# One value group a step, a fourth score bank and the maxima ahead of the copies, in the attention stage of a two-block model on one Trainium2 core

## What is computed, as far as it matters here

```python
def masked_softmax(s, mask):
    s = jnp.where(mask, s.astype(jnp.float32), -jnp.inf)
    m = jnp.max(s, axis=-1, keepdims=True)
    m = jnp.where(jnp.isfinite(m), m, 0.0)
    e = jnp.exp(s - m)
    den = jnp.sum(e, axis=-1, keepdims=True)
    return e / jnp.where(den > 0, den, 1.0)
o = gb[..., 0:1] * ocb + gb[..., 1:2] * o_sel + gb[..., 2:3] * o_win
```

## Time and profile before

| | |
|---|---|
| runs | 1525.81 us median of 3 (1525.8 to 1526.4) |
| the profiled execution | 1525.48 us, of which 1523.7 us from its first to its last instruction |
| granted TensorE clock | 1.00 |
| busy | PE 1499.2 us (98%), DVE 1067.5, ACT 697.7, POOL 272.8 |
| the stage of the change | from about 662 to 817 us of the span |
| two steps in the middle of it | 18.1 us, PE busy all of it |

### The profile page before, as it was taken

The page is one execution under the profiler, slowest core; times in us unless marked ns, Lnnn a source line. Parts: engine busy times, 40 slices in busy tenths (PEclk is TensorE's granted clock), DMA queues, the critical chain, the costliest instruction groups (busy, mean ns, idle before and its releaser), DMA issues.

```text
span 1523.7 us, 21005 instructions
## 1 busy us (share of the span) xinstructions
PE 1499.2 (98%) x8228; PEld 1247.5 (82%) x8228; DVE 1067.5 (70%) x1619; ACT 697.7 (46%) x1209; POOL 272.8 (18%) x206
## 2 busy tenths in 40 slices
PE   6999999999999999999999999999999999999999
PEld 5788888888888897987878888888888898877777
DVE  6898688889988773268885685666534653688665
ACT  4453552322314454357775552322314443777761
POOL 0110013223232000059872011111100011010000
PEclk9999999999999999999999999999999999999999
DMA  9775257468585213330000255344332342112211
GB/s 340 259 263 176 84 215 259 169 247 305 185 285 185 87 53 132 122 116 2 2 2 29 83 196 171 115 141 166 139 111 83 97 156 83 56 55 65 86 72 56
DMA packets 114248, 207.54 MB, mean 136 GB/s; under 512 B 6361, under 2 KB 21990, under 8 KB 114150
## 3 DMA queue, kind: packets, MB, share of 16 engines
q1 hardware_dynamic: 113822, 206.09, 39.4%
q10 hardware_dynamic: 328, 0.12, 0.0%
HBM read 202.00 MB, written 4.19 MB: 135 GB/s over the span
## 4 chain that ended last, share of the span: by engine, by line
PE 95%; DVE 3%; ACT 1%; issue 1%; DMA 1%; SPq 0%; ACTq 0%; DVEq 0%
PE PS L2387 56%; PE PS L2340 20%; PE PS L2743 3%; PE PS L2770 2%; PE PS L2733 2%; PE PS L2548 1%; PE PS L2839 1%; PE PS L2411 1%; PE PS L2824 1%; PE PS L2671 1%; PE PS L2905 1%; PE PS L2927 1%; PE PS L2735 1%; DVE MROW L1474 1%; DMA PIECE<-in_ada_w_dram 1%
## 5 line engine op out<-in xcount | busy, mean ns | idle before, releaser
L773 ACT ACTIVATE WH<-RAW 128x2048 fp32r<-128x2048 f32 (+1 forms) x102 | 191.2, 1885 | 340.2 <-DMA RAW<-in_ff_w_in_dram 221.2
L1353 DVE TENSOR_TENSOR WL<-RAW,WH 128x2048 fp32r<-128x2048 f32 (+1 forms) x98 | 248.9, 2563 | 74.2 <-ACT WH L773 74.1
L548 POOL PARTITION_ALL_REDUCE MROW<-MACC x25 | 118.5, 4740 | 591.1 <-DVE MACC L1388 504.2
L2387 PE MATMUL PS<-WH,HIDh 128*128 128x512 f32 (+1 forms) x576 | 217.4, 378 | 0.0
L2387 PE MATMUL PS<-WH,HIDl 128*128 128x512 f32 (+1 forms) x576 | 217.3, 377 | 0.0
L2387 PE MATMUL PS<-WL,HIDh 128*128 128x512 f32 (+1 forms) x576 | 217.3, 377 | 0.0
L2387 PE MATMUL PS<-HTh,WH 128*128 128x512 f32 (+1 forms) x520 | 202.4, 389 | 0.0
L2387 PE MATMUL PS<-HTl,WH 128*128 128x512 f32 (+1 forms) x520 | 202.4, 389 | 0.0
L2387 PE MATMUL PS<-HTh,WL 128*128 128x512 f32 (+1 forms) x520 | 202.3, 389 | 0.0
L2387 PEld LDWEIGHTS PS<-WH,HIDh 128*128 128x128 f32 x576 | 108.4, 188 | 20.5 <-issue 0.2
L2387 PEld LDWEIGHTS PS<-WL,HIDh 128*128 128x128 f32 x576 | 108.4, 188 | 20.4
(11 more groups left out here) (386 smaller groups left out, 3067.0 us busy)
## 6 DMA issues: line engine op xcount, KB each, us to landing
MRAW<-in_ada_w_dram SPq DMA_DIRECT2D x40, 1024.0 KB, 7.4
RAW<-in_ff_w_in_dram SPq DMA_DIRECT2D x32, 1024.0 KB, 5.3
RAW<-in_ff_w_out_dram SPq DMA_DIRECT2D x32, 1024.0 KB, 5.1
RAW<-in_w_in_dram SPq DMA_DIRECT2D x16, 1024.0 KB, 5.2
MRAW<-in_w_ada_dram SPq DMA_DIRECT2D x12, 1024.0 KB, 9.0
PIECE<-in_ada_w_dram SPq DMA_DIRECT2D x16, 512.0 KB, 9.7
MRAW<-in_kv_ada_w_dram SPq DMA_DIRECT2D x8, 1024.0 KB, 6.2
RAW<-in_kv_w_dram SPq DMA_DIRECT2D x6, 1024.0 KB, 5.2
```

The lines of the kernel that those rows point to most:

```text
L548: pool.partition_all_reduce(MROW[:], acc[:], P, RADD).then_inc(m_red, 1)
L773: act.activation(rounded(u)[:, 0:width(u)], RAW[:, u % 4, 0:width(u)], ACT.Copy).then_inc(w_hi, 1)
L1353: dve.tensor_tensor(WL[:, u % 4, 0:width(u)], RAW[:, u % 4, 0:width(u)], rounded(u)[:, 0:width(u)].bitcast(F32), ALU.subtract).then_inc(w_ ...
L2387: mm = pe.matmul(po, a, b_, start=(k == 0 and i == 0), stop=(k == KT - 1 and i == len(ops) - 1), skip_group_check=len(ops) > 3)
```

## The change

- `values` is called once a step, at i = 6: the compressed matmul, then all 20 products of the two branches and both tiles (40 matmul instructions), in one accumulation in bank 7. Bank 6 joins the score banks.
- Units 0 to 6 have banks 0 to 6, later ones 0, 1, 2 and 6 in turn; the scores of u wait for `exp` of u - 4.
- The ring PT has 8 buffers; the two new ones lie where QT's first two pairs were.
- COPY_LAG goes from 14 to 13, and DVE does `negmax` in front of the copy of its slot.
- The compressed mask has FLOOR in its padding column (number 31), so a row without a compressed key has a sum of 1 there. The maximum with FLOOR in L1917 and the one with 1e-30 (L1951) go; L1917 becomes a plain subtraction. POOL has one small memset more at the start.
- Near the end ACT's second conversion of weights (L773) waits for the last value group, where it waited for the compressed matmul of the last step, and stands in front of the last output's high part.

```diff
-    TURN_LAG, COPY_LAG, VALUES_LAG = 12, 14, 16
+    TURN_LAG, COPY_LAG, VALUES_LAG = 12, 13, 16
     def score_bank(u):
-        return u if u < 6 else u % 3
+        return u if u < 7 else (0, 1, 2, 6)[(u + 1) % 4]
     def summed(u):
-        return 3 * (u // PER) + (1, 2, 3, 2, 3, 3, 3)[u % PER]
+        return u // PER + 1
     def before_in_pt(u):
-        return u - PER if u % PER else u - 2 * PER
+        if u % PER == 0:
+            return u - 2 * PER
+        r = row(u) - 8
+        return PER * (r // 6) + r % 6 + 1 if r >= 0 else -1
...
             if t == UNITS + COPY_LAG:
-                act.wait_ge(a_pv, 3 * SUPER - 2)
+                act.wait_ge(a_pv, SUPER)
                 hi(2 * n.chunk + 1)
...
-                dve.scalar_tensor_tensor(out=w, in0=SM[:, 8:12, None].to_broadcast([P, 4, 32]), scalar=FLOOR, in1=w,
-                                         op0=ALU.max, op1=ALU.subtract).then_inc(a_nm, 1)
+                dve.tensor_tensor(w, SM[:, 8:12, None].to_broadcast([P, 4, 32]), w, ALU.subtract).then_inc(a_nm, 1)
...
-            dve.tensor_scalar(s_, s_, 1e-30, None, ALU.max).then_inc(a_rc, 1)
-            dve.wait_ge(a_rc, 3 * S + 1)
             dve.reciprocal(s_, s_).then_inc(a_rc, 1)
...
         for t in range(UNITS + VALUES_LAG + 2):
+            if t < UNITS:
+                negmax(t)
             if 0 <= t - COPY_LAG < UNITS and not by_act(t - COPY_LAG):
                 copy(t - COPY_LAG)
-            if t < UNITS:
-                negmax(t)
...
-            if u >= 6:
-                pe.wait_ge(a_ex, u - 2 if u >= 9 else u - 5)
+            if u >= 7:
+                pe.wait_ge(a_ex, u - 3 if u >= 10 else u - 6)
+            elif u == 6:
+                pe.wait_ge(hc_r, 3)
...
+            pe.wait_ge(*copied(PER * S))
+            if S >= 1:
+                pe.wait_ge(a_ol, S)
+            pe.matmul(PS[:, 7, 0:2 * P], VC[:, g, :], PTC[S % 2][:], start=True, stop=False, skip_group_check=True)
+            for v in range(u - 5, u + 1):
+                pe.wait_ge(*copied(v))
+            for blk, br, of in ((1, 0, (u - 5, u - 3)), (1, 1, (u - 2, u)), (0, 0, (u - 4, u - 1)),
+                                (0, 1, (u - 4, u - 1))):
...
-            elif t > VALUES_LAG and t - VALUES_LAG < UNITS and (t - VALUES_LAG) % PER in (0, 3, 6):
+            if 0 <= t - VALUES_LAG < UNITS and (t - VALUES_LAG) % PER == 6:
                 values(t - VALUES_LAG)
```

More of the change, by code:

```diff
@@ L195, in program @@
     PT = [scratch(f"PT{i}", [P, 512]) for i in range(6)]
+    PT += [at(f"PT{6 + i}", [P, 512], F32, o_y + 2048 * i) for i in range(2)]
     PBC = [scratch(f"PBC{i}", [P, P]) for i in range(2)]
@@ L569, in pool_program @@
         pool.memset(MD[:], 0.0).then_inc(pool_c, 1)
-        pool.memset(MCM[:], 0.0).then_inc(pool_c, 1)
+        pool.memset(MCM[:, :, 0:CMP], 0.0).then_inc(pool_c, 1)
         pool.memset(IDB[:], 0.0).then_inc(pool_c, 1)
@@ L575, in pool_program @@
             pool.memset(PTC[i][:], 0.0).then_inc(vc_zero, 1)
+        pool.memset(MCM[:, :, CMP:32], FLOOR).then_inc(vc_zero, 1)
         pool.wait_ge(pool_c, 8)
@@ L605, in weights @@
             if i == 1:
-                pool.wait_ge(a_rc, 3 * S + 3)
+                pool.wait_ge(a_rc, 2 * S + 2)
             for at_, br_ in parts(u):
@@ L613, in pool_program @@
         pool.wait_ge(pool_c, 11)
+        pool.wait_ge(vc_zero, 4)
         for pair in range(2):
@@ L720, in turned_of @@
     def turned_of(u):
-        return PT[row(u) % 6] if u % PER else PTC[u // PER % 2]
+        return PT[row(u) % 8] if u % PER else PTC[u // PER % 2]
     def scaled(u):
@@ L1110, in copy @@
                 act.wait_ge(a_pv, summed(before_in_pt(u)))
+            elif u > PER:
+                act.wait_ge(a_st, 4)
             p = P if u % PER else HD
@@ L1119, in out_hi @@
         def out_hi(S):
-            act.wait_ge(a_pv, 3 * S + 3)
-            act.activation(both(HIDh, S), PS[:, 6 + S % 2, 0:2 * P].rearrange("p (t c) -> p t c", c=P), ACT.Copy
+            act.wait_ge(a_pv, S + 1)
+            act.activation(both(HIDh, S), PS[:, 7, 0:2 * P].rearrange("p (t c) -> p t c", c=P), ACT.Copy
                            ).then_inc(a_oh, 1)
-        act.wait_ge(vc_zero, 3)
+        act.wait_ge(vc_zero, 4)
         for t in range(UNITS + VALUES_LAG + 1):
@@ L2752, in head @@
             def head(b, h):
[L2753 to L2763, removed]
-                pairs = ((1, 0, (u - 2, u)),) if i == 3 else ((1, 1, (u - 2, u)), (0, 0, (u - 4, u - 1)),
-                                                              (0, 1, (u - 4, u - 1)))
-                for blk, br, of in pairs:
-                    for kt in range(qts[blk] + 1):
-                        c_ = P * kt + (P * (qts[0] + 1) * br if blk == 0 else 0)
-                        for h in range(2):
-                            mm = pe.matmul(head(blk, h), VT[:, br, kt, HD * g:HD * g + HD],
-                                           turned_of(of[h])[:, c_:c_ + P], start=False,
-                                           stop=(br == 1 and kt == qts[blk]), skip_group_check=True)
+                return PS[HD * h:HD * h + HD, 7, P * b:P * b + P]
+            pe.wait_ge(*copied(PER * S))
[6 more added lines that the diff above has]
+                                (0, 1, (u - 4, u - 1))):
+                for kt in range(qts[blk] + 1):
+                    c_ = P * kt + (P * (qts[0] + 1) * br if blk == 0 else 0)
+                    for h in range(2):
+                        mm = pe.matmul(head(blk, h), VT[:, br, kt, HD * g:HD * g + HD],
+                                       turned_of(of[h])[:, c_:c_ + P], start=False,
+                                       stop=(br == 1 and kt == qts[blk]), skip_group_check=True)
             mm.then_inc(a_pv, 1)
```

17 lines of the change are left out of this document (8 added, 9 removed).

## The result

| | before | changed |
|---|---|---|
| median | 1525.5 us (1524.58 to 1526.78, 20 runs) | 1527.67 us (1526.16 to 1529.17, 20 runs) |
| ratio | | 1.0013, 95% interval 1.0007 to 1.0019 |
| profiled execution, and its span | 1525.48, 1523.7 | 1528.32, 1526.4 |

The changed kernel takes 2.2 us more. The interval excludes 1, so this small loss is real, and it is within the 0.2% taken here as no change. The forecast was 1526.2 us (1523 to 1529) and the whole range 1520.0 to 1529.5, so both hold. Some terms of the sum did less well than the sum.

The account below looks back on a forecast made before the run. PE's own work was taken as the bound, fed with nothing to spare. Start - 1.0, middle + 0.2 and end + 1.2 gave + 0.4 us, 1525.9 for the profiled execution and 1526.2 for the median; range 1520.0 to 1529.5, the forecast's own 1523 to 1529.

Parts of the forecast that it names:

- The switch and the old waits: Each step: one packed value group fewer saves 0.28 us of PE's work, and some 0.07 us of old waits is replaced.
- the compressed matmul only moves: In the value block: the compressed matmul keeps its 0.43 us and is only moved, so nothing is saved on it.
- The wait behind the block: Transposes behind the value block wait for ACT's copy, 0.5 us a step; M is the start of the mask behind the block.
- the new order does the same four things in another order, so 1.67 stays: DVE behind the block, even step: from the maxima of unit 58 to those of unit 59 stays 1.67 us.
- The middle: Twelve steps, units 23 to 107: + 0.2 us, bounds - 5 and + 3; two steps last 18.4 us.
- The start: Up to the scores of unit 23: the additional bank lets PE work earlier, - 1.0 us, bounds 0 and - 2.2.
- The end: Last products: all wait for DVE's copy, the compressed matmul's 0.43 us following; + 1.2 us, bounds + 0.3 and + 2.
- The fourth bank: Steady part: no score waits for a bank; it buys nothing alone, but keeps the block from stopping the scores.
- PE stays fed: Rival, behind the block: PE never waits; twelve steps last 104.6 us, the kernel 1520.4 us; chance 0.2.
- POOL's preparation of queries: Rival, behind the block: it holds DVE's product L1968 every second step, + 5.4 us, 1531.6 us; chance 0.12.
- the switches would stay: Rival, value block: the full-width compressed matmul stands in the group, so no switch is saved; 1526 us, chance 0.03.
- DVE's two operations: L1951 gone and L1917 cheaper, in slots where DVE runs dry: up to 0.7 us a step, priced at nothing.

Follow-up runs that it names:

- e3_lag12: The changed kernel with COPY_LAG 12 instead of 13 and DVE's copy last in its slot; 1522.65 us, ratio 0.9981 to the kernel before.
- e6_lag12_switch: e3_lag12 with each step's block cut in two by the slot's transposes, one change of the array's form more; 1526.77 us, ratio 1.0007 to the kernel before.
- e4_lag14: The changed kernel with COPY_LAG back at 14, maxima still ahead of the copies; 1546.45 us, ratio 1.0139 to the kernel before.
- e2_two: The changed kernel with the values in two groups a step, at i = 3 and i = 6; 1530.51 us, ratio 1.0034 to the kernel before.
- e1_banks3: The changed kernel with three score banks instead of four, units 0 to 6 still in banks 0 to 6; 1533.60 us, ratio 1.0056 to the kernel before.
- e7_floor_ops: The changed kernel with DVE's maximum with 1e-30 and maximum with FLOOR put back; 1528.06 us, ratio 1.0015 to the kernel before.

## Why the prediction was right, and where its steps were not

**The switch and the old waits.** Taken at 0.28 us and some 0.07, so 0.35 a step and 17.4 us for two steps without new waits. The floor is 17.42 (e3_lag12), for 18.13 before: the sum of the two is right. Both parts are real. The extra group of the kernel before costs 0.28 us, as forecast: 0.10 behind a mask, 0.15 inside, 0.03 behind the group. (e6_lag12_switch has 0.35, as its group stands between transposes.) But "the compressed matmul only moves" is not quite so: from its start to the first product it is 0.58 us in the block, of which 0.09 are the change of form, so it takes 0.49 for 0.43, and 0.22 is won a step. The old waits are 0.26 us in the two steps, before the transposes at 728.87, 731.47 and 740.70. The second, with the copy it waited for (kernel before), starts 0.16 us behind its mask instead of 0.07:

```profile
730.72 0.61 ACT L1112 ACTIVATE PT<-PS 128x512 f32<-128x512 f32 x1
731.31 0.23 PE L2735 MATMUL PS<-MD,IDB 128*128 128x128 bf16 x1
731.47 0.63 PE L2743 MATMUL PS<-IDENT,PB 128*128 128x128 f32 x4
```

**The wait behind the block.** The mechanism, its place and its releaser are as predicted. e3_lag12 takes the waits away by moving the copies one slot, and e4_lag14 makes them larger, there mostly at DVE's copies. The sizes: the odd step waits 0.62 us (0.21 + 0.41), forecast 0.42 to 0.51; the transposes start at M + 3.92 for a forecast M + 3.88, but a second, earlier wait for ACT was not seen. The even step waits 0.27, forecast 0.43 to 0.48: "the new order does the same four things in another order, so 1.67 stays" failed. They took 1.45 (735.90 to 737.35), as DVE's product took 0.41 us where it had 0.61 between the same two maxima before; M + 3.69 for M + 3.91. In the kernel before this product starts 0.06 to 0.07 us behind one of POOL's weights in four of the middle's even steps (718.37, 736.50, 754.62, 772.75) and lasts 0.61 to 0.63 us; the other products of the same size last 0.40. The chain had been read from a step in which it is long. The two errors cancel by luck: 0.89 us of waits in two steps, 18.36 - 17.42 = 0.94 by the stretches, for the 1.0 taken.

**The middle.** 18.36 for 18.4. Over twelve steps it is + 0.55 us for + 0.2, since some of the other steps wait longer than these two (the first and the last pair of the twelve last 18.53 and 18.69). Against e3_lag12, which has the same work without these waits, the waits cost 5.6 us, 0.47 a step; against that same kernel the one before is 5.05 us longer. The change wins five microseconds of PE's work and of old waits, and pays them back in new waits for copies. That answers where the gain went.

**The start.** Forecast - 1.0, measured 0. Three banks did cost here, and the wait at 673.95 is down to a half; but PE then runs into its transposes' inputs. The changed kernel's PE rows there:

```profile
674.21 0.44 PE L2739 MATMUL PS<-KDh,QS 128*128 128x384 f32 x1 [0.54 <-ACT PB L1108]
...
681.05 0.63 PE L2749 MATMUL PS<-IDENT,PB 128*128 128x128 f32 x4 [0.58 <-DVE PT L1939]
...
683.25 0.52 PE L2749 MATMUL PS<-IDENT,PB 128*128 128x128 f32 x3 [0.46 <-ACT PT L1119]
...
684.72 0.66 PE L2749 MATMUL PS<-IDENT,PB 128*128 128x128 f32 x4 [0.51 <-POOL PB L611]
```

That is 2.09 us of waits where before had 1.6 (0.29, 1.13, 0.18). What sets the length is the last of them, for POOL's weights of unit 9. It ends 21.37 us behind the mask of unit 0 in the changed kernel (684.72 - 663.35) and as late in e3_lag12 (684.00 - 662.63), where that wait is 1.13 us and the earlier ones are shorter; the start is 26.05 us in both. The whole block, 2.9 us, still lies behind that wait. In e2_two the first value group stands ahead of it, at 682.04, and covers it: PE never waits for POOL, and the start is 24.92 us, with one visit to the narrow form more than the changed kernel and as many as the one before (26.04). So the forecast's 1.0 was there to be had, and merging the groups took it back. The step that failed is "- 1.0": it asked what the scores no longer wait for, and only noted that DVE is "no less slow", without asking what PE meets next, which is POOL, and what work is left to cover that. With three banks the start of the changed kernel would be 0.7 us longer (e1_banks3), so the bank does work there.

**The end.** Forecast + 1.2, measured + 0.85. The step "the compressed matmul's 0.43 comes after them" is wrong: it waits only for its own copy and runs under DVE's last one (changed kernel):

```profile
815.78 0.65 PE L2764 MATMUL PS<-PTC,VC 128*128 128x256 f32 x2
815.98 0.56 DVE L1939 COPY PT<-PS 128x384 f32<-128x384 f32 x1 [0.37 <-PE PS L2749]
...
816.69 2.40 PE L2772 MATMUL PS<-PT,VT 128*64 128x128 f32 x40 [0.26 <-DVE PT L1939]
```

The 40 products wait 0.26 us for the copy and no more. The conversion of weights put in front of the last high part delays nothing, as the projection runs for 36 matmuls without it.

**The fourth bank** was priced at nothing in the steady part, since "it keeps the block from stopping the scores". It does, and the sum is not harmed, as the changed kernel has the bank. But what it keeps away is large, 5.9 us of the kernel and 0.9 in two steps (e1_banks3), and no row of before could show a shortage that only the block brings about. That a fourth bank beside three groups would buy nothing was not tested.

**The rivals.** "PE stays fed" did not happen but exists one slot away: its price was 17.4 us for two steps and 104.6 for twelve (6 x 17.4 is 104.4), and e3_lag12 has 17.42 at best and 105.12. POOL's preparation of queries does not hold L1968 behind the block: the same line lasts 0.41 us there in four of six even steps and 0.46 in one. It lasts longer beside POOL's weights in the last of them (792.13, 0.73 us), and there PE waits 0.60 us for 0.27 (its transposes start 0.66 behind the mask, at 794.69). So the rival was right that POOL can lengthen this chain, and wrong on when and how much. That the switches would stay is refuted by e3_lag12: PE's work in two steps is 17.42 us there, and 18.13 again when e6_lag12_switch puts one back in each step.

**DVE's two operations** cost nothing, as said (e7_floor_ops: 0.4 us of the kernel, inside the noise). What held the one with 1e-30 now holds the product behind it, see the last section; the prediction had named it as the one that would be held.

**In sum** - 1.0 + 0.2 + 1.2 was 0 + 0.55 + 0.85: 1.4 for 0.4 us. The forecast was right in its mechanism, the waits for copies behind the block; the start was wrong by 1.0 us, and an end and a middle that missed by 0.35 each, one too high and one too low, did not add to it. The rest of the median's 2.2 is not from this stage as far as the traces show. Its cause stays open: the load at the start of the program varies between kernels, and this was not tested.

## What to carry to other kernels

Work gathered into one block for PE saves its changes of form, but the engines around it run dry during the block and start again together, so a consumer that was just in time before can be late behind it: follow the chain from the end of the block and give that consumer's input an earlier place in every queue that supplies it, in all of them at once. One engine moved alone gave 0.02 and 0.15 us in two steps here, both gave 0.76. Before a wait is booked as a gain, look up what the freed engine waits for next, and whether the work that covers that wait has been moved behind it. And before the difference of two stretches is called the price of one thing, compare them start to start: short waits count as busy.

## What the runs showed of the hardware

- A visit of TensorE to the form with 64 columns and back costs 0.28 us behind a mask matmul (kernel before) and 0.35 us between transposes (e6_lag12_switch), and the profile shows it as busy time.
- Three of DVE's small operations stand in a row, and POOL's long subtractions may be running beside them. With all three (e7_floor_ops) the maximum with 1e-30 lasts 151 to 845 ns and the product with two operands in SBUF 170 to 196. Without it (changed kernel) the product is the one that is held:

```profile
760.73 0.21 DVE L1957 RECIPROCAL SM<-SM 128x12 f32<-128x12 f32 x1
760.98 0.59 DVE L1960 TENSOR_TENSOR SM<-GT,SM 128x12 f32<-128x12 f32 x1
```
```profile
758.92 2.62 POOL L601 TENSOR_TENSOR QS<-QT,QS 64x512 fp32r<-64x512 f32 x2
```

  The product starts 0.56 us before POOL's operation ends at 761.54 and ends with it (761.57). The Trainium skill (GPSIMD Engine Reference, Specifications) names the shared SBUF interfaces and operations with two SBUF inputs. The trace agrees for the product, with 590 ns for a median of 172; the reciprocal between, with one input, keeps its 0.21 us beside the same operation. The maximum with 1e-30 has one input too and was held (845 ns); which property lets it be held is not shown here. Nor is it only POOL's subtractions: DVE's product of 128x384, with one tensor input, lasts 0.61 to 0.63 us where it starts 0.06 to 0.07 us behind one of POOL's weights (kernel before, 736.50 for one), and 0.40 in its other places between 700 and 790 us.
- Transposes that wait for a copy by ACT or DVE start 0.14 to 0.15 us behind its end, in all kernels here that have such a wait.
